# Norm factors of the recurrent stage: a power on GpSimd in place of a root on ScalarE and a reciprocal on VectorE

## What is computed

```python
def rmsnorm(x, g):
    xf = x.astype(jnp.float32)
    y = xf * lax.rsqrt(jnp.mean(xf * xf, axis=-1, keepdims=True) + RMS_EPS)
    return (y * g.astype(jnp.float32)).astype(x.dtype)

    for i in range(DEPTH):
        j = i // N_MIXERS
        hn = rmsnorm(x, mix_pre_g[i])
        ...
        x = x + rmsnorm(y, mix_post_g[i])
        hn = rmsnorm(x, ffn_pre_g[i])
        y = sq_relu_mlp(hn, mlp_w1[i], mlp_w2[i])
        x = x + rmsnorm(y, ffn_post_g[i])
```

## Time and profile before

| | |
|---|---|
| median of 3 runs | 1900.45 us (1898.2 to 1900.8) |
| the profiled execution, its own time | 1899.89 us |
| its span, first to last instruction | 1898.1 us |
| TensorE (PE) busy | 1867.6 us, 98% |
| VectorE (DVE) busy | 1342.8 us, 71% |
| ScalarE (ACT) busy | 1068.3 us, 56% |
| GpSimd (POOL) busy | 89.8 us, 5% |
| recurrent stage | about 738 to 1240 us of the span |

### The profile page before, as it was taken

How to read it: one execution, slowest core, us unless ns; L and a number is a source line. 1 busy time by engine, 2 the same in 40 slices (tenths; PEclk the granted TensorE clock), 3 DMA queues, 4 the chain that set the end, 5 groups by cost and what they waited for, 6 DMA issues and landing times.

```text
span 1898.1 us, 24458 instructions
## 1 busy us (share of the span) xinstructions
PE 1867.6 (98%) x8526; PEld 1533.9 (81%) x8526; DVE 1342.8 (71%) x2120; ACT 1068.3 (56%) x1825; POOL 89.8 (5%) x121
## 2 busy tenths in 40 slices
PE   9999999999999999999999999999999999999999
PEld 6678888888888888888878888777888888888886
DVE  5877565655778987786866868777665656577885
ACT  7655555563445546766766757645655555445533
POOL 0110000000000200010000100021000000000010
PEclk9999999999999999999999999999999999999999
DMA  5344343448633533353323442245243436853353
GB/s 211 114 159 171 122 169 136 168 181 323 220 96 97 195 115 111 100 175 98 104 80 100 131 157 90 78 150 193 90 167 139 166 140 239 304 179 99 111 194 128
DMA packets 79706, 284.80 MB, mean 150 GB/s; under 512 B 9408, under 2 KB 9664, under 8 KB 71136
## 3 DMA queue, kind: packets, MB, share of 16 engines
q1 hardware_dynamic: 64288, 239.96, 36.1%
q0 software_dynamic: 8320, 27.27, 4.3%
q10 hardware_dynamic: 6976, 16.01, 2.7%
HBM read 211.31 MB, written 71.89 MB: 149 GB/s over the span
## 4 chain that ended last, share of the span: by engine, by line
PE 87%; DVE 8%; ACT 2%; issue 2%; DMA 0%; SPq 0%; DVEq 0%; ACTq 0%
PE core L1024 5%; PE core L1025 5%; PE core L1026 5%; PE bank L807 5%; PE bank L809 5%; PE bank L808 5%; PE core L974 5%; PE core L976 5%; PE core L975 5%; PE bank L1025 4%; PE bank L1024 4%; PE bank L1026 4%; PE bank L976 4%; PE bank L975 4%; PE bank L974 4%; PE bank L907 2%
## 5 line engine op out<-in xcount | busy, mean ns | idle before, releaser
L1471 ACT CAST h_hi<-h_raw 128x512 fp32r<-128x512 f32 x188 | 116.7, 621 | 230.9 <-PE core L1026 140.0
L1835 DVE TENSOR_TENSOR w_lo<-raw,w_hi 128x1024 fp32r<-128x1024 f32 x132 | 161.1, 1222 | 118.0 <-ACT w_hi L1285 115.9
L807 PE MATMUL bank<-x_hi,w_hi 128*128 128x512 f32 x560 | 224.4, 401 | 3.6 <-issue 2.9
L1285 ACT CAST w_hi<-raw 128x1024 fp32r<-128x1024 f32 x132 | 137.9, 1045 | 145.6 <-PE bank L809 45.4
L809 PE MATMUL bank<-x_hi,w_lo 128*128 128x512 f32 x560 | 218.5, 390 | 0.0
L808 PE MATMUL bank<-x_lo,w_hi 128*128 128x512 f32 x560 | 218.2, 390 | 0.0
L2092 DVE TENSOR_TENSOR h_lo<-h_raw,h_hi 128x512 fp32r<-128x512 f32 x188 | 129.5, 689 | 109.6 <-ACT h_hi L1471 109.6
L1024 PE MATMUL core<-h_hi,w_hi 128*128 128x512 f32 x464 | 180.9, 390 | 1.7 <-DVE y L2158 1.6
L1026 PE MATMUL core<-h_hi,w_lo 128*128 128x512 f32 x464 | 180.5, 389 | 0.0
L1025 PE MATMUL core<-h_lo,w_hi 128*128 128x512 f32 x464 | 180.5, 389 | 0.0
L1986 DVE TENSOR_TENSOR w_lo<-sums,w_hi 128x512 fp32r<-128x512 f32 x104 | 71.7, 689 | 96.4 <-ACT w_hi L1313 93.6
(11 more groups left out here) (334 smaller groups left out, 4375.5 us busy)
## 6 DMA issues: line engine op xcount, KB each, us to landing
raw<-weights SPq DMA_DIRECT2D x132, 512.0 KB, 3.3
h_pair_dram<-y SPq DMA_DIRECT2D x26, 1792.0 KB, 6.6
h_raw<-h_pair_dram SPq DMA_DIRECT2D x182, 256.0 KB, 2.8
w<-second_pairs SPq DMA_DIRECT2D x24, 768.0 KB, 4.5
raw_odd<-first_pairs SPq DMA_DIRECT2D x14, 1024.0 KB, 7.1
x_scratch<-y POOLq DMA_DIRECT2D x48, 256.0 KB, 2.5
raw<-first_pairs SPq DMA_DIRECT2D x12, 1024.0 KB, 7.1
xold<-x_scratch POOLq DMA_DIRECT2D x40, 256.0 KB, 3.3
```

Of the source, the lines that this page charges most:

```text
L807: nc.tensor.matmul(o, a, hi(t), start=(k == 0), stop=False)
L1285: nc.scalar.copy(w_hi[:, ROW[u] * T:(ROW[u] + 2) * T], raw[:, (n % RAW) * BLK:(n % RAW + 1) * BLK]).then_inc(hi_ready, 1)
L1835: dve.tensor_tensor(w_lo[:, s], raw[:, (n % RAW) * BLK:(n % RAW + 1) * BLK], w_hi[:, s].bitcast(F32), ALU.subtract).then_inc(lo_ready, 1)
```

## The change

Norms 6, 7, 8 and 9, those of the recurrent stage, get their factor on GpSimd, behind the sum: a multiplication by 1/1024 and an addition of epsilon in place in `tot`, then that to the power -0.5 into `rstd`. ScalarE no longer takes their roots and VectorE no longer takes their reciprocals. VectorE's waits for `rstd` and for the stores move from the tick of the reciprocal to the first use. The first column of `to_2048` holds -0.5; TensorE still waits for the three constants set before it.

```diff
-        sb("to_2048", [P, 16])
+        minus_half = sb("to_2048", [P, 16])[:, 0:1]
...
+        POWERS = (6, 7, 8, 9)
...
                 nc.gpsimd.partition_all_reduce(tot[:, :], acc[:, :], P, RADD).then_inc(tot_ready, 1)
+                if n in POWERS:
+                    pool.wait_ge(tot_ready, n - BACKGROUND + 1)
+                    pool.tensor_scalar(tot[:, :], tot[:, :], 1.0 / D, EPS, ALU.mult, ALU.add).then_inc(std_ready, 1)
+                    pool.wait_ge(std_ready, n + 1)
+                    pool.tensor_tensor(rstd[:, :], tot[:, :], minus_half.to_broadcast([P, T]), ALU.pow).then_inc(rstd_ready, 1)
...
+            pool.memset(minus_half, -0.5).then_inc(consts_set, 1)
+            pool.wait_ge(consts_set, 4)
...
-                if at in slots["root_post"]:
+                if at in slots["root_post"] and NORM_POST[chain] not in POWERS:
                     root(NORM_POST[chain])
...
-                if at in slots["root_pre"]:
+                if at in slots["root_pre"] and NORM_PRE[chain] not in POWERS:
                     root(NORM_PRE[chain])
...
-                if at in slots["recip_post"]:
+                if at in slots["recip_post"] and NORM_POST[chain] not in POWERS:
                     reciprocal_root(NORM_POST[chain])
-                    dve.wait_ge(rstd_ready, NORM_POST[chain] + 1)
...
                 for k in slots["residual"].get(at, ()):
+                    if k == 0:
+                        dve.wait_ge(rstd_ready, NORM_POST[chain] + 1)
                     chain_residual(chain, k)
...
-                if at in slots["recip_pre"]:
+                if at in slots["recip_pre"] and NORM_PRE[chain] not in POWERS:
                     reciprocal_root(NORM_PRE[chain])
-                    dve.wait_ge(rstd_ready, NORM_PRE[chain] + 1)
-                    dve.wait_ge(stored["chain"], 16 * KT * chain)
...
                 for k in slots["normed"].get(at, ()):
+                    if k == 0:
+                        dve.wait_ge(rstd_ready, NORM_PRE[chain] + 1)
+                        dve.wait_ge(stored["chain"], 16 * KT * chain)
                     chain_normed(chain, k)
```

## The result

The changed kernel takes 2176.95 us (median of 4 runs, 2175.61 to 2178.32) against 1899.99 us for the kernel before (4 runs): a ratio of 1.1454, 95% interval 1.144 to 1.1467. The direction was as forecast, the size was not: 277 us more where 38 were forecast, far beyond the top of the range.

What follows compares the result with a forecast made beforehand. TensorE was taken to bound the kernel: span 1898.1 + 32 (holds) + 8 (clock) - 2.1 (gain) = 1936.0, with run offsets 1938 us. Range 1897 to 2005 us; the forecast's own 1914 to 2005.

Steps and rivals of the forecast that it cites:

- The bound: Whole kernel bound by TensorE; in the recurrent stage it idles 16.8 us, so sparing VectorE or ScalarE gains little.
- the power's length: Each GpSimd power over 512 columns: twenty memset-like passes, 8.7 us, with ends of 0.5 and 22 us.
- rival (b): GpSimd holds VectorE and the power exceeds 22 us, each further us costing 4: above 2005 us, chance 0.14.
- both open rivals: The two cases with a power beyond 22 or 23 us, VectorE held or not: chances 0.14 and 0.03.
- The mechanism: Behind each of four sums the power stops VectorE's SBUF work, delaying a split TensorE needs: 8.0 us each, 32 us.
- the hold by a power of 4 to 22 us: The forecast's own case: GpSimd holds VectorE during each of four powers, giving 1914 to 2005 us, chance 0.47.
- what the slots could bear (23 us): Between a post norm's sum and first use of `rstd`, 24 us: an unheld power under about 23 us costs nothing.
- rival (e): VectorE not held, but a power over 23 us makes it wait for `rstd`, 4 us per us over; chance 0.03.
- The gain: After post norms 6 and 8, without the reciprocal VectorE is no longer late at `hnorm` and `w_lo`: 2.1 us.
- The queue: GpSimd's loads of old x come behind the power, 11 us early, costing nothing; over 20 us uses that up.
- The clock: Behind each of four TensorE pauses of 8 us the clock may drop: 0 to 5.5 us, taken as 2, together 8.

Runs made afterwards that it cites:

- the multiplication run: The changed kernel with a multiplication in place of the power and the scaling set to a constant: 1899.05 us, ratio 0.9989.
- four columns: The changed kernel with scaling and power on one row of the sum, brought into 128x4 and back by DMA: 1899.25 us, ratio 0.9992.
- with a logarithm: The kernel before, factors made on ScalarE by logarithm and exponential: norms 6 to 9 1899.81 us, all fourteen 1899.17 us.
- the first experiment: The kernel before with sixteen unneeded GpSimd instructions (additions, a scaling, powers of various widths) in the first MLP: 1905.59 us, one run.

## Why the prediction was wrong, point by point

**The bound was read rightly.** TensorE idle for 16.8 us in the stage said that the change could gain next to nothing, and the multiplication run lies 2.5 us below the kernel before, at the edge of its interval. The case had only a downside, and its size was the whole question.

**The step that failed first is the power's length.** Twenty passes of a memset, 8.7 us, with fifty as an upper end, 22 us. It is 82.4 us, over nine times my value and nearly four times the upper end. That a power is twenty passes was a guess, and no run shows what it computes; the runs show 0.160 us for each column. The memset row told of moving data, not of what is computed for each column, and no other row did. With a weight of 4 in the sum, and no row that bounds it from above, the end of the range should have been set by what the slots could bear (23 us) and then left open: rival (b) said only "above 2005", and I gave both open rivals together 0.17.

**The mechanism was the wrong one.** I put 0.47 on the hold by a power of 4 to 22 us and 0.03 on rival (e), a wait at the first use of `rstd` that decides from 23 us on. The hold exists: short additions about doubled VectorE's time beside them. But the power of 512 columns holds for about 2 us, as the sum does for 2.1 of 3.23. That row said it already: I quoted that the sum lets VectorE go before its end, and then carried the hold over the whole power. The rule of the Trainium skill (page "SBUF — State Buffer", section "SBUF: two separate sides") that the pair is locked for a whole instruction does not agree with these runs; 80 of 82 us are free. That the hold is the reading of the operand would fit sum and power both, and the shorter holds of the shorter powers; no run separated reading from the rest.

**Rival (e) with measured terms gives the result.** Sum's end to scaling 7.2, scaling 0.6, hand-over 0.1, power 82.4: about 90 us. VectorE comes 21.7 us after the sum's end. That leaves 68.5 us, times four 274; the late loads of old x add 2.4 for each of two, 5; the clock 10.6; less what TensorE still had to do when VectorE stopped (67.8 and 65.5 us of its own idle, not 70.9 and 68.5), 12 us; less the gain of 2. That is 276, and the span grew by 275.7.

**The 7.2 us behind each sum was missing.** It was not in the sum since in the earlier trace rows only a transfer follows the sum, at once. It shows in every run with arithmetic right behind a sum (6.8 to 7.9 us). It hides in the cover unless the rest overflows it, when it costs in full: 29 of the 277 us. The Trainium skill, page "GPSIMD Engine Reference" (Instruction dispatch), tells of about 6 us for the first call to freshly loaded code, with no instruction to be seen. The size is near; that this is the cause was not tested.

**The gain was about right in size, wrong in place.** I said that the reciprocal makes VectorE late at 839. Without it the same two idle times stand there, 0.43 and 0.52 us. What is shorter is the way between the two stops: 54.91 us from `turn_back` at 782.31 to the one at 837.22, where it was 55.47, and behind norm 8 54.96 in place of 55.80. TensorE saves it in small steps on the way, the largest, 0.4 us, at the first matmul behind the next `w_lo`, at 806 in the trace before. The runs with four columns and with a logarithm show the same within 0.1 us. That is 1.4 us. Of the 3.2 us by which the profiled spans differ, 1.3 stand ahead of the stop at 783, where both kernels do the same: part of the agreement with my 2.1 is luck. VectorE is idle at 804 to 806 in the multiplication run and then works without a real break up to `hnorm` at 836, so the backlog at 839 is made behind the reciprocal, where the residual additions run. A chain of waits almost without gaps does not say that its first link is the cause; a shorter link may be made up for by idle time further on.

**The queue.** "A power over 20 us would use that up" was right; the late load cost 2.4 us for a post norm.

**The clock.** Right that a long pause lowers it: 2.65 us each, for pauses of 64 to 68 us, against my 2 for pauses of 8. None of the runs has a pause of 8 us, but the one of 3.3 us in the first experiment lowered it too, to 0.57 over 4 us.

## What to carry to other kernels

Before moving an operation to an engine on which no trace shows it, measure that operation by itself, at its real number of columns and beside real work: no neighbouring row bounds it. When its length is unknown, name the point at which its cover ends and say what each us beyond costs, here 4, and leave the upper end open. And where an engine charges by column whatever the partitions hold, a tile with equal rows should be reshaped before the dear step: here 82 us became 1. The way there and back takes time too: the factors came 16.6 us behind the sum, which costs nothing only because that much room was there.

## What the runs showed of the hardware

- A power on GpSimd costs 0.160 us a column, whatever the exponent, the values or the number of partitions (16 or 128); an addition over 512 columns 1.52 us, a multiplication 1.04 us three times and 1.89 once.
- A power of 512 columns keeps VectorE's SBUF work waiting only for its first 2 us; additions in a row keep it waiting nearly half of the time.
- From a sum over partitions to arithmetic right behind it on GpSimd 6.8 to 7.9 us pass; a transfer from the same queue is not delayed.
- Behind a pause of 64 to 68 us TensorE starts at a granted 1.2 GHz, and on average 2.65 us are lost until it is back at 2.4. Behind pauses of 23 to 27 us 2.35 us are lost.
